# Moving the stationary activation tensors of a float32r matmul kernel to other distances from the weight buffers in SBUF

## The reference, cut to what matters

```python
h = rms_norm(x, norm1_g[l])
proj = h @ w_in[l]
qkv_g, z, b_logit, a_logit, q_s, k_s, v_s, gate_logits = jnp.split(proj, split_points, axis=-1)
y_gdn = gdn_branch(qkv_g, z, b_logit, a_logit, ...) @ w_branch_gdn[l]
y_swa = sliding_window_gqa(q_s, k_s, v_s, attn_sinks[l]) @ w_branch_swa[l]
x = x + (g_gdn * y_gdn + g_swa * y_swa) @ w_out[l]
h = rms_norm(x, norm2_g[l])
x = x + jnp.square(jax.nn.relu(h @ w_ff_up[l])) @ w_ff_down[l]
return rms_norm(x, final_norm_g)
```

## Time and profile before

| | |
|---|---|
| median of 2 runs | 1965.66 us (1962.89 to 1968.43) |
| the profiled execution | 1973.89 us |
| its span, first to last instruction | 1972.1 us |
| mean granted clock of TensorE | 0.983 of full speed |
| PE busy | 1914.2 us, 97% of the span |
| weight loads busy | 1570.8 us, 80% |
| DVE / ACT / POOL busy | 1104.9 / 883.3 / 121.6 us |
| read from HBM | 312.79 MB |

### The profile page before, as it was taken

The page is one execution under the profiler, slowest core; times in us unless marked ns, Lnnn a source line. Parts: engine busy times, 40 slices in busy tenths (PEclk is TensorE's granted clock), DMA queues, the critical chain, the costliest instruction groups (busy, mean ns, idle before and its releaser), DMA issues.

```text
span 1972.1 us, 29288 instructions
## 1 busy us (share of the span) xinstructions
PE 1914.2 (97%) x10816; PEld 1570.8 (80%) x10816; DVE 1104.9 (56%) x1470; ACT 883.3 (45%) x1398; POOL 121.6 (6%) x86
## 2 busy tenths in 40 slices
PE   7998998998998999999999999999999999999997
PEld 6887877877877888777788888888888888888886
DVE  5365675676676555656555555555554445555444
ACT  5344344344344344554444445544443334444442
POOL 0004005005014000000000000000000000000000
PEclk9898998999999999999999999999999999999998
DMA  7343333333333354344366665555555555555553
GB/s 254 112 162 116 108 125 112 108 129 118 108 128 118 115 168 138 119 139 138 128 193 202 205 201 196 194 186 188 185 192 192 192 192 182 191 182 191 193 193 127
DMA packets 87953, 316.36 MB, mean 160 GB/s; under 512 B 9648, under 2 KB 10160, under 8 KB 87728
## 3 DMA queue, kind: packets, MB, share of 16 engines
q1 hardware_dynamic: 86992, 312.64, 47.9%
q0 software_dynamic: 576, 2.10, 0.3%
q10 hardware_dynamic: 288, 0.18, 0.0%
HBM read 312.79 MB, written 2.10 MB: 160 GB/s over the span
## 4 chain that ended last, share of the span: by engine, by line
PE 54%; issue 38%; POOL 3%; DVE 3%; ACT 1%; DMA 0%; DVEq 0%; POOLq 0%; ACTq 0%; SPq 0%
PE acc L288 15%; PE acc L290 14%; PE acc L289 14%; PE J L385 4%; PE J L317 1%; PE J L433 1%; POOL rg L1406 1%; PE J L424 1%; PE J L467 1%; PE J L466 1%; PE J L441 1%; DVE qn L1043 1%; DVE cT L1043 1%; ACT w_hi L648 1%; PE J L475 1%
## 5 line engine op out<-in xcount | busy, mean ns | idle before, releaser
L988 DVE TENSOR_TENSOR w_lo<-raw,w_hi 128x1024 fp32r<-128x1024 f32 x584 | 724.7, 1243 | 672.3 <-ACT w_hi L648 670.3
L648 ACT ACTIVATE w_hi<-raw 128x1024 fp32r<-128x1024 f32 x584 | 618.4, 1060 | 654.1 <-PE acc L290 652.3
L288 PE MATMUL acc<-w_hi,hT_hi 128*128 128x512 f32 x1440 | 587.3, 408 | 12.5 <-issue 4.6
L290 PE MATMUL acc<-w_hi,hT_lo 128*128 128x512 f32 x1440 | 567.8, 394 | 0.0
L289 PE MATMUL acc<-w_lo,hT_hi 128*128 128x512 f32 x1440 | 567.2, 394 | 0.0
L288 PEld LDWEIGHTS acc<-w_hi,hT_hi 128*128 128x128 f32 x1440 | 274.0, 190 | 79.2 <-issue 15.7
L290 PEld LDWEIGHTS acc<-w_hi,hT_lo 128*128 128x128 f32 x1440 | 273.6, 190 | 59.5
L289 PEld LDWEIGHTS acc<-w_lo,hT_hi 128*128 128x128 f32 x1440 | 274.5, 191 | 52.5 <-issue 1.0
L288 PE MATMUL acc<-w_hi,act_hi 128*128 128x512 f32 x512 | 199.3, 389 | 0.0
L290 PE MATMUL acc<-w_hi,act_lo 128*128 128x512 f32 x512 | 199.2, 389 | 0.0
L289 PE MATMUL acc<-w_lo,act_hi 128*128 128x512 f32 x512 | 199.2, 389 | 0.0
(11 more groups left out here) (210 smaller groups left out, 1574.1 us busy)
## 6 DMA issues: line engine op xcount, KB each, us to landing
raw<-weights SPq DMA_DIRECT2D x584, 512.0 KB, 3.3
xres<-x SPq DMA_DIRECT2D x4, 512.0 KB, 7.4
xres<-x POOLq DMA_DIRECT2D x4, 512.0 KB, 5.6
y<-nat SPq DMA_DIRECT2D x4, 512.0 KB, 2.7
fgain_sb<-fgain SPq DMA_DIRECT2D x1, 1024.0 KB, 7.3
masks_sb<-masks SPq DMA_DIRECT2D x1, 640.0 KB, 10.6
zs<-w_ba SPq DMA_DIRECT2D x1, 256.0 KB, 9.2
dist_sb<-dist SPq DMA_DIRECT2D x1, 192.0 KB, 3.4
```

The costliest lines, as they stand in the source:

```text
L288: mm(o, aT_hi[:, kt, tok], w_hi[:, c % RING, w], start=(c == 0 and k == 0), stop=False)
L290: last = mm(o, aT_lo[:, kt, tok], w_hi[:, c % RING, w], start=False, stop=(c == nch - 1 and k == CK - 1))
L648: A(w_hi[:, slot], raw[:, slot], ACT.Copy).then_inc(hi_ready, 1)
L988: tt(w_lo[:, slot], raw[:, slot], w_hi[:, slot].bitcast(F32), ALU.subtract).then_inc(lo_ready, 1)
```

## The change

Unused tensors are put ahead of the stationary activation tensors, and `align` becomes 512 bytes smaller.

```diff
-        align = sb("align", [P, 208])
+        align = sb("align", [P, 80])
         raw = sb("raw", [P, RING, CK * NB])
         w_hi = sb("w_hi", [P, RING, CK * NB], F32R)
         w_lo = sb("w_lo", [P, RING, CK * NB], F32R)
+        gap0 = sb("gap0", [P, 64])
         hT_hi = sb("hT_hi", [P, KT, T], F32R)
+        gap1 = sb("gap1", [P, 32])
         hT_lo = sb("hT_lo", [P, KT, T], F32R)
...
         with ExitStack() as mixers:
+            gap2 = sb("gap2", [P, 16], where=mixers)
             og_hi = sb("og_hi", [P, KT, T], F32R, mixers)
+            gap3 = sb("gap3", [P, 8], where=mixers)
             og_lo = sb("og_lo", [P, KT, T], F32R, mixers)
...
             with ExitStack() as swa:
+                gap4 = sb("gap4", [P, 16], where=swa)
                 os_hi = sb("os_hi", [P, KT, T], F32R, swa)
+                gap5 = sb("gap5", [P, 16], where=swa)
                 os_lo = sb("os_lo", [P, KT, T], F32R, swa)
...
         with ExitStack() as mlp:
+            gap6 = sb("gap6", [P, 72], where=mlp)
             act_hi = sb("act_hi", [P, 32, T], F32R, mlp)
+            gap7 = sb("gap7", [P, 16], where=mlp)
             act_lo = sb("act_lo", [P, 32, T], F32R, mlp)
```

## The result

The changed kernel takes 1991.95 us (median of 2 runs, 1988.14 to 1995.77) against 1965.66 us before; the ratio is 1.0128 with a 95% interval of 1.0100 to 1.0156. So it is slower by 1.3%, 26 us, clear of the noise but under 2%. The forecast was 1966 us, and so it missed by 26 us; 1992 us lies inside the range of 1925 to 2000 only because its upper end took in rival B, whose 1990 us it nearly meets. The profiled execution took 1995.77 us with a span of 1994.0 us, 22 us more than before.

A forecast was written before the change was run, and what follows sets the result against it. PE was taken to bound the kernel through its main matmuls. The profiled execution summed to 1973.89 + 0 + 0 + 0.5 + 0 = 1974.4 us, the median to 1965.66 + 0.5, about 1966 us; range 1925 to 2000 us.

The forecast's parts named there:

- rival B: Main matmuls never settle, hi and lo at different distances: 231 ns instead of 226.7, 24 us more, 1990 us; chance 0.12.
- What bounds the kernel: PE sets the end nearly everywhere; 7008 main matmuls make 1589 of 1972 us, each nanosecond of spacing worth 7.0 us.
- Part (1): Main matmuls: distance from weight load to moving operand modulo 512 bytes changes; 0 ns taken, bounds -93 and +65 us.
- The 0.23 us ahead of L362: Spacing while PE loads `chunk_ones` at distance 128, equal to that ahead of L305 at 0; read as no effect.
- rows 7: PE timeline after four transposes: ten uneven spacings of 231 ns each, three in a row about 236, then settling.
- Parts (2) to (4): Weight split's lost larger alignment, 0; `xres` loads at a new offset, 0 to 1 us; DeltaNet tensors against `masks_sb`, 0.
- Rival C: Load and stream collide in main matmuls and this goes: 71 to 93 us less, 1884 us; chance 0.16 for over 39 us.
- Rival D: Collision of load and stream in main matmuls gets worse: some 236 ns spacing, 65 us more, 2031 us; chance 0.11.
- the 13.3 ns: Excess of each main matmul's 226.7 ns over 213.3 ns for 512 columns at full clock; 93 us in all.

The follow-up runs named there:

- e3: Kernel before with only `align` made 512 bytes smaller, no gaps, all distances 0; 1968.4 us, ratio 0.9988.
- e1: Kernel before with hi and lo of each pair at one non-zero distance (hT 256, og 448, os 32, act 160); 1988.4 us, ratio 1.0101.
- e8: Kernel before with distances of 0 and 256 mixed, hi and lo differing in three of four pairs; 1972.01 us, ratio 1.0016.
- e2: Kernel before with hi tensors at 0 and lo tensors at 128 (hT), 32 (og), 64 (os, act); 1990.38 us, ratio 1.0116.
- e6: Kernel before with `w_lo` moved to 128 modulo 512, hT at 0, act_lo and os at 128, og at 32; 1995.01 us, ratio 1.0133.
- e4: Kernel before with hi and lo alike in each pair: hT 128, og 64, os 96, act 192; 1996.7 us beside 1966.39.
- e5: Kernel before with hi and lo alike in each pair: hT 64, og 320, os 224, act 128; 2000.58 us beside 1966.39.
- e11: Kernel before with `w_lo` at 256 modulo 512, `w_hi` and all activations at 0; 1973.12 us, ratio 1.0006.
- e9: Kernel before with hi and lo alike at small distances: hT +16, og +8, os +4, act -16 bytes; 1984.03 us beside 1968.33.
- e10: Kernel before with 64 instead of 128 loaded columns in the down projection, output narrowed too; 1976.53 us beside 1968.33.
- e12: Kernel before with 32 instead of 128 loaded columns in the down projection, output narrowed too; 1981.55 us beside 1968.85.
- e7: Kernel before with `align` at 72 columns: weight buffers and activations at 480 modulo 512, all distances 0; 1970.68 us beside 1966.39.

## Why the prediction was right or wrong

**What bounds the kernel**: right. The growth of the spacing, with the matmuls behind insertions taken in (3.3 to 5.5 ns in the four pairs), adds up to the 26 us by which the time grew, 7.0 us a nanosecond. The chain and the counts are as before, and so, nearly, is the mean granted clock (0.985 after 0.983).

**Part (1), the distance**: this is the step that failed. It took 0 ns, and the runs show +4.0 ns for hT, +4.6 for og, +5.5 for os and +4.5 for act. None of the three pieces of evidence for 0 could have seen it. The 0.23 us ahead of L362 was compared with the 0.23 us ahead of L305, to 0.01 us in a question of 4 ns. In whole nanoseconds of the packed trace they are 234 (distance 128) and 231 (distance 0), and so not equal; but both are the last spacing ahead of other work, and neither is the settled 226.7. Only two of the four executions of L362 start without a wait (234 and 233 ns), against 21 of L305 (230 to 233), too few to make a price of it. That such a spacing leaves the settled value whatever is loaded should have been read as "PE is easily put out", not as "128 does nothing". L500 to L502 are paced by their loads, as the prediction itself said, so they couldn't show a stall of the stream. And slices 512 and 1024 bytes apart can't tell a period of 256. The bounds of the step, -13.3 and +9.3 ns, held. The range held because it was widened to take in rival B, not because the step was right. (The 236 ns behind +9.3 are a rounding too: the three spacings of rows 7 are 235, 233 and 236 ns, 704 in sum, 234.7 each.)

**Parts (2) to (4)**: right. e3 shows the shift of `raw` by 512 to be free (0.9988), the split kept its 1243 and 1060 ns, and the load of x went from 7.4 to 7.5 us. POOL's busy time went from 121.6 to 120.5 us. No run moves the DeltaNet's tensors alone.

**Rival B**: right in its price and wrong in its cause. It said all main matmuls would go at 231 ns instead of 226.7, 24 us, 1990 us. The numbers came out: 231.3 and 231.1 in hT and act, loss mostly in the second half. The state that it named did not: no pattern that fails to settle, but another settled one, with every spacing from 230 to 232 ns in the timeline of act. Its mean lies next to the 231 of rows 7 by luck; other distances settle at 228.9 or 233.3. And it blamed the difference between hi and lo. e1 has equal distances and a loss in three pairs, so a difference isn't needed for a loss; e8 has distances that differ by 256 and no loss. Where hi and lo differ modulo 256 (the changed kernel, e2, act in e6), each pair lost, so that as one way of losing it stands. What e1, e4, e5, e8 and e11 fit is that both streams and both loads should start at the same place modulo 256 bytes; e9 shows that this is sufficient and not strictly needed, since loads 16 bytes below the streams lose nothing. It had a chance of 0.12 where it deserved more: the uneven state in rows 7 showed that the spacing depends on how PE's streams lie to each other, and eight new distances are eight occasions to lose a state that exists at one.

**Rival C**: wrong. No distance goes below 226.7 ns in any pair. Its argument, that the excess vanishes at half clock, holds (426.7 ns before and after) but doesn't make the excess a collision; e10 and e12 speak against that, with the reserve told there. **Rival D**: wrong in size for this set. The dearest pair of the change has 232.8 ns. Equal distances come nearer to it: 234.3 at 96.

**The Trainium skill**: the page "TensorE: Matmul & The Clock Gate", Part 2, says that loading the next weights takes no SBUF read bandwidth from the running matmul. Here moving what is loaded and leaving the streams alone (the changed kernel against e3) costs 4.0 to 5.5 ns a matmul. So for float32r operands at full clock the spacing is not independent of where the load reads, and by this measurement the distance is not worth nothing. Whether it is the running stream that is held up or the start of the next matmul, no run tells.

**What stays open**: what the 13.3 ns are at distance 0, and why exactly an equal place modulo 256 with loads of 512 bytes settles. That it is a contest of load and stream for memory was only argued, and e10 and e12 speak against its simple form; that the starts must agree is shown only for the combinations of 0, 128 and 256 that were run, together with the curve above. The dip at 192, the two states at +16 and the free -16 are measured and not explained.

## What to carry to other kernels

Place the stationary and the moving operands of dense float32r matmuls with 128 loaded columns at the same offset modulo 256 bytes (the safe choice in these runs), and read the spacing of starts in the timeline, not the busy time: 226.7 against 229 to 234 ns is up to 3.4% per matmul, and the durations of the weight split on ACT and DVE don't show it. Before a spacing is used as evidence, check that it is a settled one and that it is read finely enough for the question: the last before other work and the ten behind it carry the disturbance of that work. And when a layout is varied to learn something, vary it in steps that could show the suspected period; distances that differ by multiples of 512 say nothing of 256.

## What the runs showed of the hardware

- At full granted clock a float32r matmul of 512 columns with its own load of 128 columns takes 226.67 ns from start to start in a settled stretch, and no triple of any run goes below 226.3; at half clock it takes 426.7 ns, exactly 512 columns.
- The spacing depends on the operands' places modulo 256 bytes (0 and 256 alike in e1, e8 and e11; 64 and 320, 192 and 448 alike in e4, e5 and e1), down to steps of 4 bytes (+4: 232.4 ns in os; -16: 226.7 in act), and not on the absolute address in the one shift tried (e7).
- It behaves as a property of a steady pattern and not as a sum of tolls: one load in three away from 0 costs as much as all (231.3 in both e2 and the changed kernel), one setting has two states that take turns from output to output (226.67 and 233.33 ns at +16), and a shorter load, with a narrower output, comes with a longer spacing (230.0 ns with 64 columns, 231.7 with 32).
